# Turning row tiles with scaled diagonals in the memory stage of a hybrid encoder kernel

## The reference, cut to what matters

```python
    h = num / jnp.maximum(jnp.abs(den), jnp.exp(-m_t))[..., None]
    ...
    cell = (h_f + h_b)[:, :, PAD_FRONT:].transpose(0, 2, 1, 3)
    cell = rms_norm(cell, head_norm.reshape(MLSTM_HEADS, MLSTM_HEAD_V)).reshape(bsz, l, MLSTM_WIDTH)
    o = jax.nn.sigmoid(xc @ w_ogate + b_ogate)
    hh = o * cell.astype(xc.dtype) + skip * xc
    return (hh * jax.nn.silu(z)) @ w_out
```

## Time and profile before

| | |
|---|---|
| median of 3 runs | 2712.14 us (2710.63 to 2713.55) |
| time of the profiled execution | 2708.83 us |
| span of its trace | 2707.0 us |
| TensorE busy | 2497.2 us, 92% of the span |
| VectorE, ScalarE, GpSimd busy | 53%, 36%, 42% |
| memory stage | about 1750 to 2163 us of the span |

### The profile page before, as it was taken

One profiled execution on the slowest core, in us unless ns is written; L12 is line 12 of the kernel. 1 busy time (PEld: TensorE's weight loads), 2 busy tenths in 40 slices (PEclk: granted clock), 3 DMA queues, 4 the chain that ended last, 5 costly groups with the idle time before them and its releaser, 6 DMA issues. The chain is left out here.

```text
span 2707.0 us, 40578 instructions
## 1 busy us (share of the span) xinstructions
PE 2497.2 (92%) x15206; PEld 2161.2 (80%) x15206; DVE 1435.3 (53%) x2120; ACT 975.2 (36%) x2130; POOL 1140.2 (42%) x1114
## 2 busy tenths in 40 slices
PE   6999999789998879899799999899898799999898
PEld 5988888678887679677688888787777699999787
DVE  6559887667776445405555444555555452222414
ACT  4232222756764121323232223365565420000331
POOL 3445442077775345320245354343343255554330
PEclk9999999989999889999899999999999899999999
DMA  6434443211112665535323333443434164443444
GB/s 160 107 83 132 142 147 113 103 41 41 44 44 105 161 175 162 182 111 159 100 108 128 126 120 143 156 152 125 160 106 168 68 240 157 142 142 128 168 157 155
DMA packets 271016, 349.27 MB, mean 129 GB/s; under 512 B 45652, under 2 KB 212206, under 8 KB 268406
## 3 DMA queue, kind: packets, MB, share of 16 engines
q1 hardware_dynamic: 226902, 268.59, 31.8%
q10 hardware_dynamic: 43936, 78.26, 8.1%
HBM read 223.23 MB, written 114.03 MB: 125 GB/s over the span
## 5 line engine op out<-in xcount | busy, mean ns | idle before, releaser
L1101 POOL TENSOR_TENSOR w_hi<-w_raw,ones 128x512 fp32r<-128x512 f32 (+1 forms) x232 | 289.4, 1247 | 755.6 <-PE r L1112 327.2
L1112 PE MATMUL r<-h_lo,w_hi 128*128 128x264 f32 (+1 forms) x1200 | 395.4, 330 | 7.4 <-PEq L2539 7.4
L1112 PE MATMUL r<-h_hi,w_lo 128*128 128x264 f32 (+1 forms) x1200 | 387.1, 323 | 0.0
L1112 PE MATMUL r<-h_hi,w_hi 128*128 128x264 f32 (+1 forms) x1200 | 386.4, 322 | 0.0
L1103 POOL TENSOR_TENSOR w_lo<-w_raw,w_hi 128x512 fp32r<-128x512 f32 (+1 forms) x232 | 352.0, 1517 | 18.2
L1112 PEld LDWEIGHTS r<-h_lo,w_hi 128*128 128x128 f32 x1200 | 227.1, 189 | 28.9 <-issue 9.9
L1112 PEld LDWEIGHTS r<-h_hi,w_hi 128*128 128x128 f32 x1200 | 227.1, 189 | 21.3 <-issue 2.4
L1112 PEld LDWEIGHTS r<-h_hi,w_lo 128*128 128x128 f32 x1200 | 227.1, 189 | 17.6
L467 POOL TENSOR_TENSOR w_lo<-room,w_hi 128x512 fp32r<-128x512 f32 x64 | 86.9, 1385 | 199.7 <-ACT w_hi L543 199.5
L1842 PE MATMUL o<-v,prob 116*116 116x129 f32 (+1 forms) x1296 | 166.1, 274 | 0.3 <-ACT prob L1892 0.3
L1112 PE MATMUL x<-h_lo,w_hi 128*128 128x264 f32 (+1 forms) x432 | 155.8, 361 | 6.8 <-POOL w_lo L1103 6.8
(11 more groups left out here) (384 smaller groups left out, 6201.2 us busy)
## 6 DMA issues: line engine op xcount, KB each, us to landing
w_raw<-in_w_in_even SPq DMA_DIRECT2D x72, 256.0 KB, 3.4
w_raw<-in_w_in_odd SPq DMA_DIRECT2D x64, 256.0 KB, 3.5
w_raw<-in_w_ogate SPq DMA_DIRECT2D x64, 256.0 KB, 2.9
v_d<-vs ACTq DMA_DIRECT2D x8, 1152.0 KB, 4.2
us<-u_d SPq DMA_DIRECT2D x16, 520.0 KB, 5.6
xc_d<-xc ACTq DMA_DIRECT2D x8, 1040.0 KB, 6.6
qk_d<-qk ACTq DMA_DIRECT2D x16, 520.0 KB, 2.7
qk<-qk_d SPq DMA_DIRECT2D x8, 1040.0 KB, 5.0
```

The costliest lines, as they stand in the source:

```text
L1101: self.nc.gpsimd.tensor_tensor(hi, raw, one, ALU.mult).then_inc(self.hi_done, 1)
L1112: ins = self.nc.tensor.matmul(bank[:, 0:n], w[:, u % self.buffers, k, :], z[:, off:off + n], start=(first and k == 0 and w is self.hi and ...
```

## The change

The rows are no longer scaled. Instead, ScalarE writes nine diagonal matrices per head, the identity times the row factors of a tile, and a turn becomes an ordinary float32 product of the row tile with its diagonal, which turns and scales at once. The diagonals lie in `sw`, `qs` and `qe`, which nobody uses in these slots; for that reason the queries of a head (ScalarE) and the scaled queries (GpSimd) of its first tile wait for the turns of the head before. VectorE keeps the inversion of the root, in slot 1. ScalarE makes the diagonals in slots 2, 3 and 4, behind the weighing of its slot.

```diff
+        diags = [(sw, qs)[t // 4][:, t // 2 % 2, t % 2, :] for t in range(N)] + [qe[:, 0, 0, :]]
...
-                            last = nc.tensor.transpose(dst, hs[0:m, t, f * P:(f + 1) * P], c["ident"][0:m, 0:m])
+                            last = nc.tensor.matmul(dst, hs[0:m, t, f * P:(f + 1) * P], diags[t][0:m, 0:m],
+                                                    start=True, stop=True)
...
                     if t == 0:
                         act.wait_ge(bml, 16 * (j + 1))
+                        if j:
+                            act.wait_ge(turned, 3 * j)
...
+                def scale(j, n):
+                    act.wait_ge(inverted, j + 1)
+                    act.wait_ge(h_made, NT * (j + 1))
+                    for t in GROUPS[n]:
+                        m = TILES[t][1]
+                        ins = nc.scalar.activation(diags[t][0:m, 0:m], c["ident"][0:m, 0:m], ACT.Copy,
+                                                   scale=rstd[0:m, t:t + 1])
+                    ins.then_inc(scaled, 1)
...
-                    for k in range(SLOTS if j < MH else 2):
+                    for k in range(SLOTS if j < MH else 5):
...
+                        if j and 2 <= k < 5:
+                            scale(j - 1, k - 2)
                         if j == MH - 1 and 1 <= k <= KC:
                             high(k - 1)
...
                     if t == 0:
                         gp.wait_ge(qkl, 16 * (j + 1))
+                        if j:
+                            gp.wait_ge(turned, 3 * j)
...
-                def scale(j, n):
-                    if n == 0:
-                        dve.wait_ge(root_done, j + 1)
-                        dve.wait_ge(sq_done, NT * (j + 1))
-                        do(v.reciprocal(rstd[:, :], rstd[:, :]))
-                    for t in GROUPS[n]:
-                        m = TILES[t][1]
-                        ins = v.tensor_scalar(hs[0:m, t, :], hs[0:m, t, :], rstd[0:m, t:t + 1], None, ALU.mult)
-                    ins.then_inc(scaled, 1)
+                def invert(j):
+                    dve.wait_ge(root_done, j + 1)
+                    v.reciprocal(rstd[:, :], rstd[:, :]).then_inc(inverted, 1)
...
-                        if j and 1 <= k < 4:
-                            scale(j - 1, k - 1)
+                        if j and k == 1:
+                            invert(j - 1)
```

More of the change, by code:

```diff
@@ L2499, in mlstm_z @@
         hf_done, hs_done, sq_done = s.sem("hf_done"), s.sem("hs_done"), s.sem("squares_done")
-        root_done, scaled, turned = s.sem("root_done"), s.sem("h_scaled"), s.sem("h_turned")
+        root_done, inverted = s.sem("root_done"), s.sem("root_inverted")
+        scaled, turned = s.sem("diagonals_scaled"), s.sem("h_turned")
+        diags = [(sw, qs)[t // 4][:, t // 2 % 2, t % 2, :] for t in range(N)] + [qe[:, 0, 0, :]]
         tanh_done, z_read = s.sem("tanh_done"), s.sem("z_read")
```

## The result

The changed kernel takes 2717.88 us in the median of 11 runs (2714.77 to 2720.13), the kernel before 2710.63 us (2707.63 to 2713.97). The ratio is 1.0023, with a 95% interval of 1.0015 to 1.0032: 6 us slower, where +1.9 us was forecast (the two medians are 7.3 us apart). The difference is small, but the interval doesn't contain 1, so it is a real loss.

What follows compares the result with a forecast made beforehand. TensorE was taken as the bound, with some 40 us of holes and half-speed stretches. Price 13.3 plus 0.1 behind the last cell less gain 11.5 made +1.9 us, median 2714.0 us, range 2708 to 2722, no measurable change.

Steps and rivals of the forecast that it cites:

- the price: TensorE's 18 turns per head become products: 1.9 us per head, paid in seven places, not head 7; 13.3 us.
- the gain: Without VectorE's scalings ahead of it, the add of slot 2 comes sooner, shortening waits at update 3 and half-speed stretches: 11.5 us.
- The waits left at update 3: TensorE's waits there: near 0 in heads 1 and 3; 2.1, 0.9, 1.5, 3.3 us in heads 2, 4, 5, 7.
- ScalarE's diagonals hide: Nine diagonals per head, 2.9 us on ScalarE, fit under TensorE's slots; only 0.1 us shows, behind the last cell.
- twice, not four times: A float32 product on TensorE takes two passes of a turn, adding 0.11 us per full turn; fourfold would give +25 us.
- The rivals of a cheap and of a fourfold product: Product costs no more than a turn: -11.5 us, 2700.7, chance 0.08; or four times a turn: +25 us, 2739, chance 0.03.
- some 0.1 us: Addition per head for the two small turns on TensorE, which become two records instead of one.
- So I take it that it stays up: Head 2: TensorE's clock stays at full speed behind the remaining 2.1 us wait, giving 3.0 us.
- The rival, with a chance of 0.15: Clock falls in head 2 all the same, or somewhere new: 3.0 us of gain gone, +4.9 us, 2717; chance 0.15.
- Nothing: Head 7 gains nothing: the add waits for slot 1's split anyway, so the 3.28 us wait and clock behind it stay.
- the first rival: Clock falls in head 2 all the same, or somewhere new: +4.9 us, 2717; chance 0.15.
- the price's range: With the ends of the product's price, 12.6 to 17.6 us, the whole change comes to +1.2 to +6.2 us.

Runs made afterwards that it cites:

- e1: Kernel before with each head's 18 turns made float32 products with the plain identity, VectorE's scalings kept; ratio 1.0051, +14 us.
- e2: Kernel before without VectorE's nine scalings per head and nothing in their place, rows turned unscaled; ratio 0.9954, -12.5 us.
- e5: Kernel before with VectorE's three groups of scalings one slot later, each behind its slot's add; ratio 0.998, -5.5 us.
- e4: Changed kernel with the 14 projection steps behind the last cell split 6, 4, 4 instead of 4, 5, 5; ratio 1.0006.
- e6: Changed kernel with ScalarE scaling the rows in place instead of making diagonals, turns as transposes again; ratio 0.9965, -9.5 us against the kernel before.
- e3: Changed kernel with ScalarE's weighing for update 3 ahead of the tanh in slot 2 of heads 1 to 7; ratio 1.0005.
- e8: Changed kernel, diagonals kept, with the weighing ahead of the tanh in slot 2 and projection steps split 6, 4, 4; ratio 1.0005.

## Why the prediction was right in its range and short in its size

**Right: what is bounded by what.** TensorE bounds the stage; the price is paid in full in heads 1 to 6 and behind the last cell and not in head 7 (e1), and the gain is the add of slot 2 (e2, and e5, which has it without a single instruction less). The waits left at update 3 came out nearly as written: none in heads 1 and 3, 2.12, 0.88, 1.48 and 0.77 us in heads 2, 4, 5 and 6. ScalarE's diagonals hide: 0.99 us for three, and no wait for them in heads 1 to 7.

**Right: twice, not four times.** A product is two records and 0.223 us, a transpose one and 0.108 (six in 1.34 and in 0.65 us). The Trainium skill ("TensorE: Matmul & The Clock Gate", Terms) has float32 four times as fast in the transpose mode; this case's rows do not agree, and go by two. The rivals of a cheap and of a fourfold product are out. (The fourfold rival's 2739 has the 1.9 us of the forecast in it twice: 2712.1 + 25 is 2737.) Price and gain measured alone, +14 and -12.5 us, make +1.5 us, near the +1.9 us forecast, and in the stages of the traces +17.8 and -13.3 us, that is +4.5. The whole came out at +6.2 us by the run times and +5.3 in the stage. The 4.7 us between +1.5 and +6.2 are within what the three intervals allow together (some 3.4, 3.5 and 2.3 us to either side); how much of them is the clock, the run times can't say.

**Short: the price's size.** 2.16 us per head instead of 1.9, the step "some 0.1 us" for the two small turns, which cost 0.32: +1.8 us in seven heads.

**Wrong: the step "So I take it that it stays up".** It rested on one row, the turns behind 2.00 us of waiting (the first group behind the last cell, not the last group). The rival, with a chance of 0.15, is what happened in head 2, by about half of its 3.0 us. In 14 places of the twelve traces TensorE waits 2.00 to 2.43 us, at update 3 of head 2 or behind the last cell. They are head 2 in both traces of the changed kernel and in e2, e4, e5 and e6, and the turns behind the last cell in both traces of each kernel and in e1, e3, e5 and e6. In 12 of them the clock fell for some 3.4 us, which costs 1.7 us; in two it didn't, and these are head 2 of e2 and the very row that I had read. Behind the waits of 1.4 to 1.9 us in heads 5, 6 and 7 it fell in none of the traces, and with those of 2.5 us and more it fell in all. So head 2 keeps 1.7 us of its loss, and behind the last cell the changed kernel's products stand at half speed where the first trace before had none: +1.7 us each against the forecast. In the second trace before, the part behind the last cell is 1.6 us longer than in the first for the same reason, so this part of the difference lies in the execution I read and not in the change.

**Head 7: right, though the first pair of traces hides it.** "Nothing" is 1.2 us less in that pair (60.4 and 59.2 us), at a shorter half-speed stretch behind its wait. The second trace before has 59.2 us too, so this difference isn't the change's.

**The terms.** +1.9, +1.8 for the price, +1.7 and +1.7 for the clock, -1.2 for head 7 give +5.9 us; the stage shows +5.3. The 0.6 us are heads 1, 4 and 6, which gained 0.15 to 0.26 us each more than forecast. The second pair of traces shows +5.1 us by other terms: head 4 gives 1.3 us more and the part behind the last cell costs 1.6 less, while head 0, which the change doesn't touch, costs 1.2 and head 7 gives nothing.

**Luck.** The measured 2717.9 us is nearest the number of the first rival, 2717, and +6.2 us is the upper end of the price's range. Neither is a hit: half of the rival's term came, and the rest is a price sized too low, a fall of the clock behind the last cell that the sum didn't have, and an execution taken as the base whose head 7 was long and whose turns behind the last cell were fast.

**What stays open.** Of the six traces with products, four (e1, e3, e4, e8) have one more fall of the clock in head 1, behind the waits of slot 8, which costs 1.6 us; both traces of the changed kernel and all six with transposes have none. These waits (0.45 us at update 8 and 1.28 us at the score behind it) are the same in both. So a fall can come behind waits shorter than 2 us as well. Why the clock falls in one and not in the other no run isolates, nor whether it falls in the executions without a profile; the run times of e3, e4 and e8 can't be read to 1.6 us for that reason.

## What to carry to other kernels

Folding a scale into a transpose is not free: on TensorE a float32 product with a diagonal takes twice the time of the transpose, 2.16 us per head here, and where TensorE is the bound that is the whole price. What the change gained came from where one instruction stood in VectorE's list, and reordering alone gave 5.5 us (e5), and moving the scalings to a less busy engine 9.5 us (e6). Before a wait or a stretch at half speed is counted as gone or as kept, it should be read in more than one execution.

## What the runs showed of the hardware that was not expected

- A wait of 2.0 to 2.4 us on TensorE came with a fall to half speed in 12 of 14 cases, for some 3.4 us; the same program had it in one execution and not in the next (before: behind 2.00 us, 1.00 and then 0.60 in a 4 us window).
- Two float32 products of 16 x 16 outputs took 0.54 us, more than two of 128 x 128 (0.45 us); as transposes they took 0.22 us.
